# Second block's experts: down weights issued by ScalarE on its own DMA queue

## The reference

```python
def hier_moe_2(h, w_rg, b_rg, w_re, b_re, w_gate, w_up, w_down):
    ...                                   # routing: two experts per token, with their weights in combine
    y = jnp.zeros_like(hf)
    for e in range(N_EXPERTS_2):          # 32 experts
        he = jax.nn.silu(hf @ w_gate[e]) * (hf @ w_up[e])      # [512,1024] @ [1024,256], twice
        y = y + combine[:, e:e + 1] * (he @ w_down[e])         # [512,256] @ [256,1024]
    return y.reshape(B, S, D)
```

## Time and profile before

| | us |
|---|---|
| median of three runs | 1530.0 |
| the profiled execution, whole | 1528.88 |
| its span, first to last instruction | 1527.0 |
| first `gate_up` of the second block's experts starts | 1252.56 |
| last `gate_up` (tile 31) starts | 1490.05 |
| last `down` (tile 31) starts | 1496.18 |

### The profile page before, as it was taken

The page is one execution under the profiler, slowest core; times in us unless marked ns, Lnnn a source line. Parts: engine busy times, 40 slices in busy tenths (PEclk is TensorE's granted clock), DMA queues, the critical chain, the costliest instruction groups (busy, mean ns, idle before and its releaser), DMA issues. The chain is left out here.

```text
span 1527.0 us, 20419 instructions
## 1 busy us (share of the span) xinstructions
PE 1298.0 (85%) x7696; PEld 1040.5 (68%) x7696; DVE 704.5 (46%) x1271; ACT 462.1 (30%) x1011; POOL 422.7 (28%) x358
## 2 busy tenths in 40 slices
PE   7997789949999249899999999999798939987872
PEld 6776567849999238779989988788676725543441
DVE  5787773634434465663745537571233341111112
ACT  4542343123332154442242332523323211111110
POOL 5355211211110214212414234135244013322213
PEclk9999879959999769999999999999899959999896
DMA  6300350169995503101213121322121889999995
GB/s 261 111 0 1 134 197 31 55 266 380 385 377 197 181 30 120 61 1 61 78 62 110 56 84 61 107 83 83 56 100 43 349 329 383 388 383 386 398 390 205
DMA packets 65430, 266.53 MB, mean 175 GB/s; under 512 B 8484, under 2 KB 18340, under 8 KB 52400
## 3 DMA queue, kind: packets, MB, share of 16 engines
q1 hardware_dynamic: 54320, 237.92, 41.3%
q0 software_dynamic: 9216, 20.99, 4.1%
q10 hardware_dynamic: 1792, 6.29, 1.2%
HBM read 244.13 MB, written 31.52 MB: 181 GB/s over the span
## 5 line engine op out<-in xcount | busy, mean ns | idle before, releaser
L1703 POOL TENSOR_TENSOR block_w_lo<-block_w,block_w_hi 128x512 fp32r<-128x512 f32 x96 | 130.5, 1361 | 218.2 <-ACT block_w_hi L1681 218.2
L2357 PE MATMUL e_gu<-e_w,e_xT 128*64 128x256 f32 x1024 | 130.3, 412 | 28.4 <-DMA e_w<-in_gu 27.6
L2357 PEld LDWEIGHTS e_gu<-e_w,e_xT 128*64 128x64 f32 x1024 | 77.3, 149 | 71.8 <-DMA e_w<-in_gu 30.3
L240 PE MATMUL dil_bank<-block_w_hi,xT_hi 128*128 128x512 f32 x288 | 116.4, 404 | 4.3 <-PEq L828 4.3
L1681 ACT ACTIVATE block_w_hi<-block_w 128x512 fp32r<-128x512 f32 x96 | 60.4, 631 | 181.3 <-PE dil_bank L242 116.0
L241 PE MATMUL dil_bank<-block_w_lo,xT_hi 128*128 128x512 f32 x288 | 114.5, 398 | 0.0
L242 PE MATMUL dil_bank<-block_w_hi,xT_lo 128*128 128x512 f32 x288 | 114.4, 397 | 0.0
L240 PEld LDWEIGHTS dil_bank<-block_w_hi,xT_hi 128*128 128x128 f32 x288 | 77.6, 269 | 8.5 <-issue 4.7
L2418 DVE TENSOR_TENSOR e_prod<-e_sg,e_gu 128x128 f32<-128x128 f32 x32 | 9.2, 288 | 158.2 <-ACT e_sg L2449 158.2
L241 PEld LDWEIGHTS dil_bank<-block_w_lo,xT_hi 128*128 128x128 f32 x288 | 77.8, 270 | 3.8
L242 PEld LDWEIGHTS dil_bank<-block_w_hi,xT_lo 128*128 128x128 f32 x288 | 77.6, 269 | 4.0
(11 more groups left out here) (501 smaller groups left out, 3144.4 us busy)
## 6 DMA issues: line engine op xcount, KB each, us to landing
e_w<-in_gu SPq DMA_DIRECT2D x48, 2048.0 KB, 18.1
e_w<-in_dn SPq DMA_DIRECT2D x48, 1024.0 KB, 19.7
block_w<-in_w_dil SPq DMA_DIRECT2D x9, 2048.0 KB, 8.0
block_w<-in_w_out SPq DMA_DIRECT2D x4, 2048.0 KB, 9.3
block_w<-in_w_gates SPq DMA_DIRECT2D x4, 2048.0 KB, 9.2
w_t<-in_w_in_t SPq DMA_DIRECT2D x12, 512.0 KB, 3.2
slot_rows<-blank SPq DMA_DIRECT2D x12, 512.0 KB, 6.5
slot_rows<-e_y ACTq DMA_DIRECT2D x16, 384.0 KB, 8.6
```

The lines of the kernel that those rows point to most:

```text
L240: pe.matmul(out, lhs[0], rhs[0], start=first, stop=False)
L1703: pool.tensor_tensor(wl[:, j % RING, 0:width[i]], k.w[:, (q0 + i) % 2, c, 0:width[i]], wh[:, j % RING, 0:width[i]].bitcast(F32), ALU.subtr ...
L2357: ins = pe.matmul(gubank[t % 2][g * S:(g + 1) * S, 0:2 * FG], xT[t % 2][:, c * S:(c + 1) * S], w1[slot.of[t]][:, w:w + 2 * FG], start=(c = ...
```

## The change

SyncE no longer loads the down weights of tiles 7 to 31, and no longer waits for `y_done` there (both stay in the branch for tiles past 32, which the measured input doesn't take). ScalarE issues w2[t+7] right behind its copy of tile t's output. It has waited for `y_done` of that tile by then, which is what says that slot's down weights have been read.

```diff
@@ -2286,8 +2286,9 @@
                     b, u = slot.of[t], slot.last[t]
                     sp.wait_ge(gu_done, u + 1)
                     sp.dma_start(w1[b][:], w_gu[bass.ds(e, 1)].rearrange("a p n -> (a p) n")).then_inc(w1_in[b], 16)
-                    sp.wait_ge(y_done, u + 1)
-                    sp.dma_start(w2[b][:], w_dn[bass.ds(e, 1)].rearrange("a p n -> (a p) n")).then_inc(w2_in[b], 16)
+                    if t >= E:
+                        sp.wait_ge(y_done, u + 1)
+                        sp.dma_start(w2[b][:], w_dn[bass.ds(e, 1)].rearrange("a p n -> (a p) n")).then_inc(w2_in[b], 16)
 
                 sp.wait_ge(x_in[0], 16)
                 late(sp)
@@ -2441,6 +2442,9 @@
                     if t >= 2:
                         act.wait_ge(y_out[t % 2], 16 * (t // 2))
                     act.activation(y[t % 2][:], ybank[t % 2][0:U, :], ACT.Copy).then_inc(y_s, 1)
+                    if t + R < E:
+                        b = slot.of[t + R]
+                        act.dma_start(w2[b][:], w_dn[t + R]).then_inc(w2_in[b], 16)
 
                 def tile(t, more):
                     act.wait_ge(gu_done, t + 1)
```

## The result

The changed kernel takes 1561.2 us (median of 4 runs, 1553.9 to 1564.36), the one before 1530.8 on the same chip: a ratio of 1.0196, 95% interval [1.0174, 1.0218]. It is slower by 30 us where 1531.5 was forecast, 25 us above the end of the range. The profiled execution is the fastest of the four, 1553.9 us with a span of 1552.0. From the first `gate_up` of the stage to the last it takes 1514.14 - 1247.93 = 266.2 us, against 1490.05 - 1252.56 = 237.5 before: +28.7 us.

The account below looks back on a forecast made before the run. The DMA engines were taken as the limit, the end hanging on w1[31]. Terms 0 + 0 + 1.3 + 0 took 1528.88 to 1530.2; with 1.1 for the median and 0.2 for the clock, 1531.5 us, range 1527.5 to 1536.5.

Parts of the forecast that it names:

- What bounds the kernel: In the stage, DMA engines always full; TensorE sets 6.38 us a tile until tile 16, then loads set 8.95.
- SyncE's wait removed: SyncE's loads without the wait for y_done: earlier issue only waits longer in a full queue, worth 0.
- ScalarE's 25 issues: Down loads issued on ScalarE, about 0.3 us each, fit into its 3.26 us idle a tile: worth 0.
- Two queues: the order: At the stage's end, w1 and w2 alternate by packets, 2 to 1 in bytes; w1[31] lands half a load, 1.3 us, later.
- The rate: DMA rate over the stage with weights in two queues: unchanged, 0; bounds 7 us loss and 4.5 us gain.
- The hope that thinned-out gathers might raise the rate: A third queue halving the gathers' slow stretches could raise the mean DMA rate some 2%, 4.5 us gained.
- The stage's end: The kernel's end hangs on w1[31] landing, forecast at 1491.2; tile 31's gate_up starts at about 1491.3.
- The clock: TensorE's lower clock might fall on the last tile after an idle microsecond: 0.2 us added.
- Down weights run ahead: Queues share by bytes, so the last loads are all w1 and tile 31 starts 3.5 to 5.0 us later; chance 0.17.
- Fall behind: ScalarE's queue gets under every second turn, so the last down loads land late: +1.5 to +4.9 us; chance 0.12.
- The signs named for a wrong prediction: w2 tiles ahead, TensorE waiting for loads before tile 16, down waits, rate over 2% from 393, ScalarE issues of several us.

Follow-up runs that it names:

- two to one: Changed kernel with gate and up loads in halves (8 KB packets) and down loads in halves (4 KB), against the kernel before: 1534.89 us, ratio 1.0027.
- 8 against 8 KB: Changed kernel with each gate and up load as two transfers of half the columns, 8 KB packets, against the kernel before: 1537.87 us, ratio 1.0039.

## Why the prediction was wrong

*What bounds the kernel.* Right for the kernel before: the loads bound it from tile 16 on. But the prediction named two limits, TensorE at 6.38 us a tile and the loads at 8.95, and not the third, GpSimd's gathers and scatters. With two buffers a gather has at most two tiles' time, 12.8 us at the fast pace; its 8.6 us (7.1 to 9.6) fitted into that, 15 to 19 us don't.

*SyncE's wait removed: 0.* Right within the noise: with wait and order changed in one queue, 0.9986 [0.9970, 1.0002]. SyncE's long issues went as said.

*ScalarE's 25 issues: 0.* Right for the length of an issue, 0.33 us each. The issues alone cost at most 0.3%.

*Two queues: the order, +1.3 us.* The turns by packets were right, and so was 2 to 1 between the weights: 2567 packets to 2533. This is the step that failed, by what it left out. It took q10's turns from q1 alone. GpSimd's queue was the other party in the earlier trace rows, with 35 packets to q1's 36. Of three queues that are all full, each gets a third. Nothing was charged for the gathers and scatters, whose turns became dearer by an 8 KB packet each. The sum that was missing needs one count more from the trace before, the 165 packets a tile of GpSimd's queue. A round of one 16 KB and one 8 KB packet is 24 KB; at 385 GB/s these are 0.064 us, or 15.7 rounds a microsecond, and 165 packets a tile would take 10.5 us, against 8.95 for the loads. Measured were 17.6 packets a microsecond and 9.32 us a tile. That q0's packets are mostly tiny does not help: a turn is a turn. Where the third queue's share was repaired ("two to one"), the last `gate_up` was 1.4 us late, close to the term. That is partly luck: the stage is one execution, and w2[31], which the same step had in time by 2.5 us, came 2.56 us too late.

The Trainium skill (DMA: Bandwidth & Descriptors, Queues, rings and completion order) has a DMA engine go round the queues that have work. The trace agrees, and that rule with a third queue in it would have said this. Its packets of some 9 to 17 descriptors fit less well, if a descriptor is a row: the trace of the changed kernel has mostly one 16 KB row to one 8 KB row to one small one. Of some 1640 packets under 512 B on GpSimd's queue between 1300 and 1460, 55% have a 16 KB packet of q1 start 5 to 7 ns behind their own start, where chance would give 4%. (The packets bear no engine's number, so this is read from their times alone.)

*The rate: 0.* Nearly right: 381 GB/s against 388 between 1300 and 1460, 7 GB/s less in all, 6 of them the gathers' and scatters' (4.86 against 5.80 MB in 160 us). The hope that thinned-out gathers might raise the rate was the sentence that came closest to the fault. It saw that a third queue slows the gathers down, and asked only what this does to the rate, not who waits for a gather. Two slips in this part's arithmetic change nothing in the forecast: 128 packets in 8.95 us are 14.3 turns a microsecond and not 16 (6 us at most, not 7), and a gain of 2.5% gives 1525.9, while 1527.2 belongs to 1.9%.

*The stage's end.* Wrong, for the same reason. w1[31] landed at 1463.2 + 18.6 = 1481.8, where the forecast had 1491.2 (of the difference, 4.6 us are the earlier start of the stage), and nobody wanted it: tile 31 started at 1514.14. The cushion of slots loaded ahead, which before was used up by tile 16, was never used up here. When w1[31] landed, five tiles' gate and up weights lay unread (tiles 27 to 31), and TensorE had to work through them while the DMA engines fell idle.

*The clock: 0.2.* Wrong in size. The granted clock was 0.89 from 1260 to 1355 (1.00 before), and longer matmuls make up 12.7 us of the 28.7.

*The rivals.* None was this one. "Down weights run ahead" was priced at 3.5 to 5 us and measured, in the kernel that brings it about (8 against 8 KB), at 6 us by the ratio and 9.2 in the stage. The price counted one interval of 5.2 us, where w2 is three tiles ahead. With three it would have been 5.9 us, or 7.6 with a tile at the low clock (1492.4 - 15.6, and three tiles of TensorE behind it). "Fall behind", priced at 1.5 to 4.9 us, showed 5.9 in the stage when w2 was held back two tiles by its issue, which is another way to come late than losing turns. The signs named for a wrong prediction were partly met. TensorE waited before tile 16, but for gathers, which were not on the list. From 1355 to 1480 the rate was 382 GB/s, 2.8% under the 393 of before, past the 2% named as a sign; no issue on ScalarE was long.

## What to carry to other kernels

Where the DMA engines are full, a second full queue does not take from the first alone: it takes turns from every queue, and the one with many small packets pays most. What it pays is the length of the others' packets: a third queue of 64 B packets did not delay the gathers (8.7 us). Before a load is moved to another queue, list all queues that have work at that time, count the packets a tile needs from each, and divide by the turns it will get. If a gather beside bulk loads is late, keep the bulk in one queue or cut its packets; deeper buffers only lengthen the wait.

## What the runs showed of the hardware

- A packet under 512 B costs its queue as much as one of 16 KB: a turn. It costs the others hardly anything: 2857 packets of ScalarE's queue, all of 64 B or less, took 1.4% of the DMA engines' time. Between 1300 and 1460 GpSimd's queue moved 1/11 of the bytes of the weights (4.86 against 55.9 MB) with over a third of all packets.
- A transfer queue fills up. With all weights, or with two pieces a tile, on ScalarE's queue an issue held the engine up to 12.4 us; in the changed kernel, with at most seven loads there, it stayed under 0.4 us.
- The clock's loss moves with the idle time: before, `gate_up` paid for it (412 ns a matmul against 393 after), now `down` does (605 ns before, 751 after).
- In one queue, packets of 4 KB moved the weights in the same time as packets of 16 and 8 KB (1.0008 [0.9989, 1.0027]).
